# Gate products spread over the position-bias stage of a two-block transformer kernel

## The reference

```python
proj = h @ w_in[l]
(aq, ak, av, iq, ik, iw, bq, bf, bi, bg, cq, ckv, ckpe, gate_logits) = jnp.split(proj, split_pts, axis=-1)
o_a = dsa_attention(...)   # 4 heads, 128 of up to 512 keys chosen per token, with a position bias
o_b = hgrn2_mixer(...)
o_c = mla_attention(...)   # 4 heads, all keys before the token
gates = sigmoid(gate_logits)               # (512, 3072)
mixed = g_a * (o_a @ w_up_a[l]) + g_b * (o_b @ w_up_b[l]) + g_c * (o_c @ w_up_c[l])
```

## Time and profile before

| | us |
|---|---|
| median of 3 runs | 1465.45 (1462.56 to 1466.1) |
| span of the profiled execution, first to last instruction | 1458.1 |
| TensorE busy | 1381.3 (95%) |
| VectorE busy | 960.8 (66%) |
| ScalarE busy | 535.1 (37%) |
| GpSimd busy | 69.3 (5%) |

### The profile page before, as it was taken

How to read it: one execution, slowest core, us unless ns; L and a number is a source line. 1 busy time by engine, 2 the same in 40 slices (tenths; PEclk the granted TensorE clock), 3 DMA queues, 4 the chain that set the end, 5 groups by cost and what they waited for, 6 DMA issues and landing times.

```text
span 1458.1 us, 18976 instructions
## 1 busy us (share of the span) xinstructions
PE 1381.3 (95%) x7108; PEld 1077.4 (74%) x7110; DVE 960.8 (66%) x1634; ACT 535.1 (37%) x882; POOL 69.3 (5%) x50
## 2 busy tenths in 40 slices
PE   6999999999997798999999999999999999999889
PEld 5759898866665566888888788888769854566677
DVE  6558688876767657764556755643499758568773
ACT  6457434533225633243323322432223221214421
POOL 0000000000005400000000000000000011201000
PEclk9999999999998899999999999999899999989999
DMA  6213111132211214542344334232422213530001
GB/s 252 73 58 114 49 69 60 58 108 99 87 51 51 74 51 152 176 171 87 116 162 156 145 145 157 78 120 80 132 64 93 87 58 87 176 113 1 1 1 58
DMA packets 40891, 141.05 MB, mean 97 GB/s; under 512 B 13280, under 2 KB 17632, under 8 KB 28768
## 3 DMA queue, kind: packets, MB, share of 16 engines
q1 hardware_dynamic: 35616, 131.05, 25.4%
q10 hardware_dynamic: 5184, 8.78, 1.7%
HBM read 128.94 MB, written 8.39 MB: 94 GB/s over the span
## 4 chain that ended last, share of the span: by engine, by line
PE 76%; DVE 16%; ACT 3%; DMA 3%; issue 2%; DVEq 0%; ACTq 0%; SPq 0%; another core or an unknown queue 0%
PE turn L734 21%; PE score L734 17%; PE score L719 9%; PE sum L734 9%; PE sum L719 5%; DVE ring_r L1967 3%; DMA ring<-wstream 3%; PE turn L963 2%; PE score L872 2%; PE sum L1316 1%; DVE work L1967 1%; ACT heads_r L1424 1%; PE score L1198 1%; DVE rows L1973 1%; PE sum L894 1%
## 5 line engine op out<-in xcount | busy, mean ns | idle before, releaser
L1967 DVE TENSOR_TENSOR ring_r<-ring,heads_r 128x1024 fp32r<-128x1024 f32 (+2 forms) x161 | 186.1, 1156 | 186.4 <-ACT heads_r L1424 183.4
L1424 ACT ACTIVATE heads_r<-ring 128x1024 fp32r<-128x1024 f32 (+2 forms) x161 | 161.9, 1006 | 139.4 <-PE turn L734 70.3
L734 PE MATMUL score<-h_sb_r,heads_r 128*128 128x512 f32 x368 | 146.4, 398 | 0.0
L734 PE MATMUL turn<-tiles_r,heads_r 128*128 128x512 f32 x368 | 143.2, 389 | 0.0
L734 PE MATMUL turn<-h_sb_r,heads_r 128*128 128x512 f32 x336 | 131.0, 390 | 1.0 <-DVE work L1973 1.0
L734 PE MATMUL score<-x_sb_r,heads_r 128*128 128x512 f32 x224 | 94.7, 423 | 1.8 <-DVE ring_r L1967 1.8
L734 PE MATMUL score<-x_sb_r,ring_r 128*128 128x512 f32 x224 | 89.7, 400 | 0.0
L734 PEld LDWEIGHTS score<-h_sb_r,heads_r 128*128 128x128 f32 x368 | 70.6, 192 | 12.8 <-DVE tiles_r L1967 0.2
L734 PEld LDWEIGHTS turn<-tiles_r,heads_r 128*128 128x128 f32 x368 | 69.1, 188 | 14.2
L734 PEld LDWEIGHTS turn<-h_sb_r,heads_r 128*128 128x128 f32 x336 | 63.1, 188 | 15.4 <-DVE work L1973 1.4
L734 PE MATMUL turn<-wide_r,heads_r 128*128 128x512 f32 x188 | 73.1, 389 | 0.0
(11 more groups left out here) (463 smaller groups left out, 3112.5 us busy)
## 6 DMA issues: line engine op xcount, KB each, us to landing
ring<-wstream SPq DMA_DIRECT2D x91, 1024.0 KB, 4.9
ring<-wstream SPq DMA_DIRECT2D x16, 704.0 KB, 4.4
ring<-gated SPq DMA_DIRECT2D x6, 1024.0 KB, 6.5
gated<-tiles ACTq DMA_DIRECT2D x18, 256.0 KB, 2.0
ring<-wstream SPq DMA_DIRECT2D x4, 840.0 KB, 4.9
x_sb<-xT SPq DMA_DIRECT2D x4, 512.0 KB, 7.8
x_sb<-xT ACTq DMA_DIRECT2D x1, 2048.0 KB, 7.6
ring<-wstream SPq DMA_DIRECT2D x3, 512.0 KB, 3.5
```

The lines of the kernel that those rows point to most:

```text
L734: return pe.matmul(out, a, w, **k) if moving else pe.matmul(out, w, a, **k)
L1424: step(act.activation(head_piece(p), chunk(name)[:, c:c + cols], ACT.Identity), f"head {p}")
L1967: step(dve.tensor_tensor(out, a, b, op), name)
```

## The change

The gates that run in the bias stage become five (17 to 21) instead of three. Their 40 k-tiles are spread over all 32 eighths: two after each of the eighths 0 to 7, one after each later one. The dsa attention keeps gates 22 and 23, in four half gates after items 0, 4, 8 and 12. ScalarE no longer calls `beside` in the bias stage: after the masks of eighth i it drains the gates that are complete before eighth i-3 and makes the heads of those that start by eighth i+3. VectorE makes the rests one to two eighths ahead, behind the steps. Three waits of TensorE ahead of the loop go; eighths 0 and 1 still wait for the banks that they write.

```diff
 PLACES = [(f"rank {i}", 2) for i in range(8)] + ... + \
-         [("latent 0", 2), ("latent 1", 4)] + [(f"mla {i}", 1) for i in range(18)] + [(f"bias {i}", 1) for i in range(6)] + \
-         [(f"dsa {i}", 1) for i in range(8)]
+         [("latent 0", 2), ("latent 1", 4)] + [(f"mla {i}", 1) for i in range(18)] + [(f"bias {i}", 2) for i in range(5)] + \
+         [(f"dsa {i}", 1) for i in range(4)]
+BIAS_GATES, DSA_AT = 5, (0, 4, 8, 12)
+FINE = len(GATES) - len(DSA_AT) // 2 - BIAS_GATES
+BESIDE_BIAS = [2] * 8 + [1] * 24
+def gate_before(i):
+    return sum(BESIDE_BIAS[:max(i, 0)]) // KD
@@ split_units (TensorE)
-    ... "each" if tag == "gate" and 17 <= 2 * i + e < 20 else True):
+    ... "each" if tag == "gate" and FINE <= 2 * i + e < FINE + BIAS_GATES else True):
@@ TensorE, bias stage
             pe.wait_ge(dve_step, at("increments"))
-            pe.wait_ge(turn_done, tally.count["turn_full"])
-            pe.wait_ge(score_done, tally.count["score_full"])
-            pe.wait_ge(sum_done, sums[0])
...
-                if 4 <= i < 28:
-                    run(units, 1)
+                run(units, BESIDE_BIAS[i])
...
-                      beside=lambda i: i < 16 and i % 2 == 0 and beside(f"dsa {i // 2}"))
+                      beside=lambda i: i in DSA_AT and beside(f"dsa {DSA_AT.index(i)}"))
@@ ScalarE, bias stage and dsa
             for i in range(4, len(EIGHTHS)):
-                if i < 28 and i % 4 == 0:
-                    beside(f"bias {i // 4 - 1}")
                 signs(i)
+                drains(units_before(PLACE["bias 0"]) + gate_before(i - 3))
+                weight_heads(upto=max(made[0], pieces_through(PLACE["bias 0"] + gate_before(i + 3))))
...
-                if i % 2 == 0:
-                    beside(f"dsa {i // 2}")
-                elif i < 8:
+                if i in DSA_AT:
+                    beside(f"dsa {DSA_AT.index(i)}")
+                if i % 2 and i < 8:
                     head(f"out {5 + i // 2}", OUT_HEAD[5 + i // 2], TL[:, 5 + i // 2, :])
-                elif i in (11, 13):
+                if i in (11, 13):
                     weight_heads()
@@ VectorE, bias stage and dsa
             for i, (key, o) in enumerate(EIGHTHS):
-                if 4 <= i < 28 and i % 4 == 0:
-                    beside(f"bias {i // 4 - 1}")
                 if 2 <= i + 1 < len(EIGHTHS):
                     steps(i + 1)
+                weight_rests(upto=max(rested[0], pieces_through(PLACE["bias 0"] + gate_before(i + 2))))
...
-                if i < 16 and i % 2 == 0:
-                    beside(f"dsa {i // 2}")
+                if i in DSA_AT:
+                    beside(f"dsa {DSA_AT.index(i)}")
```

More of the change, by code:

```diff
@@ L136 @@
 PLACES = [(f"rank {i}", 2) for i in range(8)] + [(f"rec {h} {l}", 1) for h in range(4) for l in range(LEVELS + 1)] + \
-         [("latent 0", 2), ("latent 1", 4)] + [(f"mla {i}", 1) for i in range(18)] + [(f"bias {i}", 1) for i in range(6)] + \
-         [(f"dsa {i}", 1) for i in range(8)]
+         [("latent 0", 2), ("latent 1", 4)] + [(f"mla {i}", 1) for i in range(18)] + [(f"bias {i}", 2) for i in range(5)] + \
+         [(f"dsa {i}", 1) for i in range(4)]
 PLACE = {n: i for i, (n, _) in enumerate(PLACES)}
 assert sum(k for _, k in PLACES) == len(BESIDE)
+BIAS_GATES, DSA_AT = 5, (0, 4, 8, 12)
+FINE = len(GATES) - len(DSA_AT) // 2 - BIAS_GATES
+BESIDE_BIAS = [2] * 8 + [1] * 24
+assert len(BESIDE_BIAS) == 32 and sum(BESIDE_BIAS) == KD * BIAS_GATES
+def gate_before(i):
+    return sum(BESIDE_BIAS[:max(i, 0)]) // KD
 ADA_AT = [j for j in range(2, 20) if j % 3]
@@ L765, in split_units @@
                         b = gemm_bank()
-                        for mm in split_tile(b[:, :], f"{tag}_{i}", e * KD * P, acts, ready if i + e == first else None, "each" if tag == "gate" and 17 <= 2 * i + e < 20 else True):
+                        for mm in split_tile(b[:, :], f"{tag}_{i}", e * KD * P, acts, ready if i + e == first else None, "each" if tag == "gate" and FINE <= 2 * i + e < FINE + BIAS_GATES else True):
                             if mm is None:
```

## The result

| | before | after |
|---|---|---|
| median, us (4 runs each) | 1464.59 (1462.56 to 1466.1) | 1443.33 (1438.41 to 1446.66) |
| ratio, 95% interval | | 0.9862 (0.9842 to 0.9881) |
| span of the profiled execution | 1458.1 | 1444.9 |

The change makes the kernel 1.4% faster: 21.3 us by the medians. The direction and the two places of the gain were right. From the entry of the bias stage to the end of dsa the two profiled executions differ by 17.6 us (544.35 against 561.60 at the end, and the changed kernel had entered the bias stage 0.4 us later). Their whole spans differ by only 13.2 us. These three numbers, 21.3, 13.2 and 17.6, are what the runs had to reconcile.

What follows compares the result with a forecast made beforehand. The prediction saw no engine full in the bias stage, TensorE waiting for ScalarE's masks and VectorE, and TensorE as dsa's bound. Gains 4.0 + 1.6 + 9.4 = 15.0 us off 1458.1 gave 1443.1, plus 7.35 made 1450.5 us; range 1445 to 1459.

Steps and rivals of the forecast that it cites:

- The step that failed: Final sum: the 7.35 us between profiled span and median of three runs is added to 1443.1, giving 1450.5 us.
- bias stage: Position bias stage: mask waits go and gaps fill, so dsa begins at 498.0 instead of 502.9; -4.0 us after allowance.
- first half gate of dsa, clock: Head of dsa: k-tiles in the last eighths keep the clock up, 2.75 us instead of 4.39; -1.6 us.
- rest of dsa: dsa: four half gates leave, 11.0 us, less 0.4 us of uncovered latency for each; -9.4 us.
- block-by-block sum: Bias stage: the slowest engine's time in each of four key blocks, 16.1, 13.3, 9.8 and 7.2, together 46.4 us.
- 0.9 us given back for unevenness: Bias stage: allowance for three near-equal engines handing work over in short rings; cuts the gain from 4.9 to 4.0 us.
- latency uncovered by each half gate: dsa: score, maximum, exponential and transposes chain exposed where a half gate leaves; 0.4 us each, bounds 0 and 2.75.
- Rival 1: Bias stage stays as long because VectorE, ScalarE and TensorE hold each other up; 1454.5 us, chance 0.15.
- rival 2: dsa: each removed half gate exposes a whole maximum and exponential, 1.4 us; 1454.5 us, chance 0.12.
- rival 3: Cover lost in both stages and low clock stays at the bias stage's entry, costing 2.4 us; 1461 us, chance 0.07.
- Rival 4: Clock falls in the thinned dsa; 1453.5 us for six us of it, 1456.5 for twice that; chance 0.06.
- Rival 5: Low clock holds through the bias stage, TensorE needing 70.2 us there; slower at 1474.6 us, chance 0.05.

Runs made afterwards that it cites:

- c_before2: The kernel before, unchanged, profiled a third time; 1462.53 us in one run.
- c_before: The kernel before, unchanged, run once more for a second profile; median 1463.75 us.
- e_items: The changed kernel with its four half gates of dsa after items 2, 6, 10 and 14 instead of 0, 4, 8 and 12; median 1443.19 us.
- e_order: The kernel before with only ScalarE's order changed in the bias stage: masks first, each gate drained four eighths later; median 1453.55 us, ratio 0.9937.
- e_ahead: The changed kernel with ScalarE draining each gate ahead of the next masks, as the kernel before did; median 1452.06 us.
- e_one: The changed kernel with each gate drained behind the masks of one further eighth instead of four; median 1446.88 us.
- e_waits: The changed kernel with the three removed TensorE waits put back ahead of the bias loop; median 1441.92 us.
- c_after: The changed kernel, unchanged, run once more for a second profile; median 1443.79 us.
- e_early: The kernel before with drains behind the masks and its 24 k-tiles after eighths 0 to 23 instead of 4 to 27; median 1454.67 us.

## Why the prediction was wrong, point by point

**The step that failed** is the last of its sum: "The median of three runs is 1465.45, 7.35 above the profiled span; the profile gives no other time of its own execution, so I carry that distance along." The step is wrong because a distance of 7.35 us between a profile and a median is not a constant of the kernel. 1.8 us of it lie around every span. The other 5.5 are how far this one execution was ahead of the median set against it. Where one such difference lies was seen: c_before2 lost 2.9 us to c_before in one longer fall behind 1295 us; the rest lies in no profiled execution. With 1.8 us the same sum gives 1458.1 - 15.0 + 1.8 = 1444.9, and the range would begin at 1439.6; measured are 1443.33 and 1443.79. Of the 7.2 us by which the forecast was missed, 5.5 are this step. The rest is the terms, 2.6 us too small together, less about 1 us that the changed kernel's median execution was slower outside the two stages than the profile of before. The terms alone would not have missed the range: 1465.45 - 17.6 is 1447.9.

Why the changed kernel's median did not keep the distance is only half known. By an estimate (median, less 1.8, less the end of dsa in the profiles), the kernel before needs 900.0 us behind dsa in its median execution and the changed one 897.4, where the program is the same. So by the medians some 2.6 us were gained behind the two stages, where nothing was changed. Between c_before and c_before2, one kernel, a single late fall made 2.9 us. Whether the change makes them rarer or the eight executions were lucky stays open.

**The terms**, measured between the same instructions:

| term | forecast | measured |
|---|---|---|
| bias stage | -4.0 | -5.1; -6.5 without the fall at 481 |
| first half gate of dsa, clock | -1.6 | -1.6 (4.39 to 2.81) |
| rest of dsa | -9.4 | -11.0 (58.7 to 46.1, less 1.6) |
| sum | -15.0 | -17.6 |

- *Bias stage.* My block-by-block sum gave a first dsa score at 498.0, 48.3 us behind the transposes; it came at 498.23, 48.1 us behind them. That near agreement is partly luck, since the sum has no fall in it and the stage had one of 1.4 us. At full clock (e_items, 46.7) the sum was 1.6 us too long, and the 0.9 us given back for unevenness made it worse.
- *ScalarE.* Shown: the order caused the waits (e_order, e_ahead), and a store of four eighths instead of one is worth 2.6 us (e_one). The removed waits are worth the 0.7 us given (e_waits).
- *dsa.* 0.4 us for the latency uncovered by each half gate was too much. Four half gates gave back 11.0 of 11.0, six give 16.4 of 16.5 and eight 21.4 of 22.0, each counted from 57.1. The row that I took it from, 0.55 us at the tail, is a wait that stood there already; the removed half gates covered next to none. TensorE is not busy for 6.6 of 59.1 us in dsa before, for 6.6 of 46.6 after and for 6.5 of 35.7 with seven gates. The waits for the exponential hardly grew, 2.1 us where the earlier trace rows have 2.0:

```profile
PE turn L895 <- ACT probs L1412: 2.1, 4, 0.8
```

- *The rivals.* Rival 1 (no gain in the stage) and rival 2 (latency comes out in dsa) are refuted by the stage columns, and rival 3 with them: the granted clock was 1.00 from 457 to 463. Rival 4, the clock falling in a thinned dsa, didn't happen with four half gates, two or none. It was the one for which the Trainium skill spoke ("TensorE: Matmul & The Clock Gate", section "A second HAM failure mode: psum-queue depth-cycling"), where frequent short idles between groups of matmuls make the clock of another kernel swing; dsa, busy for 82% at a granted clock of 1.00, does not behave so here, and the measurement decides. Rival 5 didn't come: with denser k-tiles the mean granted clock of the stage was 0.96 instead of 0.80.
- *What I didn't see.* The gain of the whole kernel needs the clock behind the changed stages too. From the end of dsa to the end of the span the changed kernel took 4.1 us longer than the kernel before in the first pair of profiles and 2.0 us longer in c_after. Of these, 0.9 us lie in one wait of TensorE for a weight piece near 806 us, 2.4 and 2.5 us long in the changed kernel's two profiles and 1.5 in the same place before; it is 1.7 in e_items and e_waits. Behind 1100 us the changed kernel had 17.1 and 10.2 us of low clock, the kernel before 10.2, 6.8 and 17.1 in its three profiles. Single profiles can't rank the two kernels there.

What the change does, then: of 17.6 us, 8.4 are the order of the drains (e_order, the clock in the stage and at the head of dsa included), and 9.2 are the rest. These are two gates moved from a stage where TensorE is the bound to one where it has time to spare (11.0 out of dsa, 1.8 into the bias stage, from which the 0.7 of the three removed waits is already taken off).

## What to carry to other kernels

An engine that drains filler work should make first what the main line wants next, with as many buffers in store as the drain can make it wait; with four eighths of masks TensorE did not wait for them here, with one the stage was 2.6 us longer. Filler belongs where the engine that runs it is not the bound, and it pays to go on moving it until the stage that receives it grows by as much as the other shrinks: six or seven gates instead of five are 4.5 and 5.0 us faster still by the medians. From a profile to a forecast carry only the time that lies around every span, and know where the profiled execution stands among the others before you set it against a median.

## What the runs showed of the hardware

Falls of the granted clock may come or not with the same program up to that point: at 481 us in after and c_after, and not in e_items. In all the profiles read here they last 3.4, 6.8, 10.2 or 13.7 us. What a fall costs goes by what bounds the stretch: one of 3.4 us at 504 cost 1.6 us where TensorE was the bound (4.39 against 2.81 for the first half gate), and with one of 10.2 us gone from an entry where VectorE was the bound the stage was only 1.3 us shorter (e_order, e_early, which differ in the place of the k-tiles too).
